# An FFN's up projection by seven block products instead of eight, with weight sums from accumulating DMAs and from VectorE

## The reference

```
def swiglu(x, w_in, w_out):
    gate, up = jnp.split(x @ w_in, 2, axis=-1)
    return (jax.nn.silu(gate) * up) @ w_out

h = swiglu(rmsnorm(x, g[0]), lw['ffn_in'][0], lw['ffn_out'][0])
x = x + FFN_RES * rmsnorm(h, g[1])
```

## Time and profile before

| | us |
|---|---|
| median of 3 runs (lowest, highest) | 2800.34 (2798.26, 2802.26) |
| the profiled execution | 2801.57 |
| its span, first to last instruction | 2799.8 |
| TensorE busy | 2723.5 |
| VectorE busy | 1254.4 |
| ScalarE busy | 888.7 |
| GpSimd busy | 383.1 |

### The profile page before, as it was taken

One profiled execution on the slowest core, in us unless ns is written; L12 is line 12 of the kernel. 1 busy time (PEld: TensorE's weight loads), 2 busy tenths in 40 slices (PEclk: granted clock), 3 DMA queues, 4 the chain that ended last, 5 costly groups with the idle time before them and its releaser, 6 DMA issues.

```text
span 2799.8 us, 45262 instructions
## 1 busy us (share of the span) xinstructions
PE 2723.5 (97%) x18703; PEld 2610.4 (93%) x18703; DVE 1254.4 (45%) x1697; ACT 888.7 (32%) x1213; POOL 383.1 (14%) x350
## 2 busy tenths in 40 slices
PE   8999999999899999999999999999989999999999
PEld 8999999997679999999999999999966899999998
...
DMA packets 367939, 191.19 MB, mean 68 GB/s; under 512 B 36477, under 2 KB 363472, under 8 KB 367822
## 3 DMA queue, kind: packets, MB, share of 16 engines
...
## 4 chain that ended last, share of the span: by engine, by line
PE 90%; DVE 5%; ACT 3%; issue 2%; DMA 0%; DVEq 0%; ACTq 0%; SPq 0%
PE ps L600 26%; PE ps L601 26%; PE ps L602 26%; PE ps L895 2%; PE ps L904 1%; PE ps L1023 1%; DVE w L1820 1%; PE ps L955 1%; ACT w L1323 1%; PE ps L1001 1%; DVE at L2118 1%; PE ps L937 1%; PE ps L1002 0%; DVE mx L2086 0%; DVE y L1913 0%
## 5 line engine op out<-in xcount | busy, mean ns | idle before, releaser
L600 PE MATMUL ps<-xh,w 128*128 128x320 f32 x3456 | 1076.3, 311 | 20.1 <-DVE xl L1897 13.3
L601 PE MATMUL ps<-xl,w 128*128 128x320 f32 x3456 | 1070.8, 310 | 0.0
L602 PE MATMUL ps<-xh,w 128*128 128x320 f32 x3456 | 1070.8, 310 | 0.0
L600 PEld LDWEIGHTS ps<-xh,w 128*128 128x128 f32 x3456 | 651.4, 188 | 29.5 <-DVE xl L1897 20.4
L601 PEld LDWEIGHTS ps<-xl,w 128*128 128x128 f32 x3456 | 651.7, 189 | 0.3
L602 PEld LDWEIGHTS ps<-xh,w 128*128 128x128 f32 x3456 | 651.4, 188 | 0.0
L1820 DVE TENSOR_TENSOR w<-raw,w 128x2048 fp32r<-128x2048 f32 x172 | 401.9, 2336 | 367.4 <-ACT w L1323 367.3
L1323 ACT ACTIVATE w<-raw 128x2048 fp32r<-128x2048 f32 (+2 forms) x185 | 342.6, 1852 | 414.6 <-PE ps L602 406.8
L600 PE MATMUL ps<-hh,w 128*128 128x320 f32 x1408 | 436.9, 310 | 1.0 <-DVE w L1820 1.0
L602 PE MATMUL ps<-hh,w 128*128 128x320 f32 x1408 | 435.1, 309 | 0.0
L601 PE MATMUL ps<-hl,w 128*128 128x320 f32 x1408 | 435.1, 309 | 0.0
...
## 6 DMA issues: line engine op xcount, KB each, us to landing
...
y<-in_cache_ckv_dram POOLq DMA_DIRECT2D x8, 256.0 KB, 3.2
```

The lines of the kernel that those rows point to most:

```text
L600: pe.matmul(out, wh, xh, start=first, stop=False)
L601: pe.matmul(out, wh, xl, start=False, stop=False)
L602: return pe.matmul(out, wl, xh, start=False, stop=last)
```

## The change

The up projection is cut into block products. For 128 columns, the weights of gate and up and the two halves of the features form a 2 x 2 matrix of blocks: A11 and A12 are gate's features 0 to 511 and 512 to 1023, A21 and A22 those of up (each 128x512 in SBUF). The activations form the other: features by token halves. `strassen_unit` computes the four results (gate and up, by token half) from seven products of blocks instead of eight, each 4 chunks x 3 = 12 matmuls of 128x320, so 84 for a unit instead of 96. In this it needs four sums of weight blocks and four combinations of activation blocks.

- *Weight sums.* S3 = A21 + A11 is made in RAW and S1 = A21 + A22 in SB (into which SP loads A21 once more), both by accumulating DMAs from SBUF to SBUF that GpSimd issues (`summed`). S2 and S4 are made on VectorE (`block_sum`). `group_hi` and `group_lo` split the seven blocks (3584 columns where a unit had 2048) in five groups: A11; S1 and S2; A12 and S3; A22; S4. Events: `ss_sb` for a sum, `ph_sb` for a high part, `pl_sb` for a low part, `pd_ps` for a product, `pc_sb` for a copy, `pu_sb` for VectorE's three steps on the results.
- *Results.* Products 1, 3 and 5 run up in bank b = 4j+1, where ScalarE first copies product 1, from PSUM to PSUM (COPY_P1); it copies the state of b behind products 3 and 5 out to GB and UB. Bank c takes product 2 and, once VectorE has made C22 = c + UB from it, product 7. The second half of gate is finished after product 7, in the next unit: gate_2, gate_2_r, Silu, `gated` (the product of both, with its sign), `high_h` (the copy into HH), `low_h`.
- *Activations.* `g_of_x` puts gain x X of four chunks into Y on ScalarE, behind r. `combined` makes three combinations and T4 from it on VectorE in units 1 and 2 of the plain part, split into TC; T4 is split into XH and XL (`fourth_hi`, `fourth_lo`) during the following down units. R is no longer applied to up: in the plain part the eviction of up multiplies with Silu's output, in place of two instructions.
- *Parts.* An FFN is now 4 plain up units and 8 down units over 4 chunks, then three times 6 block-product units and 8 down units over 6 chunks. All down parts start both of their first units before the last hidden chunk is there. The down weights of units 0 and 1 are split ahead. In the last down unit the sums of squares stand two chunks before its end instead of four.
- *Norm.* SY starts from a term for epsilon that ScalarE computes (`seed_y`) ahead of the last down units, instead of from GpSimd's memset; the logarithm takes no bias.
- Some semaphores of the mixers are merged.

```diff
-UP_A, UP_B = 12, 10
+PARTS = (4, 6, 6, 6)
+HT, HMAX = sum(PARTS), max(PARTS)
...
+QUARTERS = KD // 2
+BLK = QUARTERS * P
+PRODUCTS = ((0, True), (2, True), (1, False), (0, False), (1, False), (3, True), (2, False))
+LASTP = len(PRODUCTS) - 1
+GROUPS = (slice(0, 1), slice(1, 3), slice(3, 5), slice(5, 6), slice(6, 7))
+FREED_BY = (0, 2, 4, 5)
+G_A11, G_S12, G_A12S3, G_A22, G_S4 = range(5)
+STRASSEN = HT - PARTS[0]
+COPY_P1, COPY_U2, COPY_U3 = range(3)
+GATE_1, C22, C21 = range(3)
...
+            if blocks is not None:
+                for q in range(2 * pairs):
+                    i, j, g = q // 2, q % 2, blocks + q
+                    at = (first + q) * P
+                    load(unit(l, base, i, j), j,
+                         [(RAW[:, j, r * 1024:(r + 1) * 1024].rearrange("p (k n) -> p k n", n=P),
+                           src[:, :, at + r * DFF:at + r * DFF + P]) for r in range(2)])
+                    if q:
+                        sp.wait_ge(*pl_sb.nth(l, 4 * (g - 1) + G_S12))
+                    sp.dma_start(SB[:, 0, :].rearrange("p (k n) -> p k n", n=P),
+                                 src[:, 0:QUARTERS, at + DFF:at + DFF + P]).then_inc(loads_in, 16)
+                return
...
+        def strassen_unit(l, u, j, g):
+            pe.wait_ge(drained, u + 1)
+            for s, (bank, fresh) in enumerate(PRODUCTS):
+                if s == 0:
+                    pe.wait_ge(*pl_sb.nth(l, 4 * g + G_A11))
+                if s == 1:
+                    pe.wait_ge(*pl_sb.nth(l, 4 * g + G_S12))
+                if s == 2:
+                    pe.wait_ge(*pc_sb.nth(l, 3 * g + COPY_P1))
+                if s == 3:
+                    pe.wait_ge(*pl_sb.nth(l, 4 * g + G_A12S3))
+                if s == 4:
+                    pe.wait_ge(*pc_sb.nth(l, 3 * g + COPY_U2))
+                if s == 5:
+                    pe.wait_ge(lo_ready, u + 3)
+                if s == 6:
+                    pe.wait_ge(*pl_sb.nth(l, 4 * g + G_S4 - 1))
+                    pe.wait_ge(*pu_sb.nth(l, 3 * g + C22))
+                for k in range(QUARTERS):
+                    mm = three(PS[:, 4 * j + bank, 0:HALF], *slot_w(s, k), *product_x(s, k),
+                               fresh and k == 0, k == QUARTERS - 1, True)
+                mm.then_inc(unit_done if s == LASTP else pd_ps.sem, 1)
...
+        def strassen_up(l, f, p, base):
+            at, n = base + PART_AT[p], PARTS[p]
+            h0 = f * HT + sum(PARTS[:p])
+            def gate_2(q):
+                act.wait_ge(*gate_ready.nth(l, h0 + q))
+                run(GB[:, q % 2, N2], GB[:, q % 2, N2], ACT.Silu).then_inc(silu_ready.sem, 1)
+            for q in range(n):
+                j, g = q % 2, strassen(f, p, q)
+                more = q + 1 < n
+                b = PS[:, 4 * j + 1, 0:HALF]
+                if q:
+                    group_hi(l, at, q, g, G_S4)
+                act.wait_ge(*pd_ps.nth(l, LASTP * g))
+                run(b, PS[:, 4 * j, 0:HALF], ACT.Copy).then_inc(pc_sb.sem, 1)
+                if q:
+                    gate_2(q - 1)
+                if more:
+                    group_hi(l, at, q + 1, g + 1, G_A11)
+                if q:
+                    high_h(l, 1 - j, q - 1, h_ready.nth(l, g - 1))
+                act.wait_ge(*pd_ps.nth(l, LASTP * g + 2))
+                act.wait_ge(*hl_ready.nth(l, h0 + q - 2))
+                run(GB[:, j, N2], b, ACT.Copy).then_inc(pc_sb.sem, 1)
+                if more:
+                    group_hi(l, at, q + 1, g + 1, G_S12)
+                else:
+                    split_hi_d(l, at + n, 0, 0, n)
+                act.wait_ge(*pd_ps.nth(l, LASTP * g + 4))
+                run(UB[:, j, N1], b, ACT.Copy).then_inc(pc_sb.sem, 1)
+                act.wait_ge(*pu_sb.nth(l, 3 * g + GATE_1))
+                run(GB[:, j, N1], GB[:, j, N1], ACT.Silu)
+                if more:
+                    group_hi(l, at, q + 1, g + 1, G_A12S3)
+                    group_hi(l, at, q + 1, g + 1, G_A22)
+                else:
+                    split_hi_d(l, at + n, 0, 1, n)
+            gate_2(n - 1)
+            high_h(l, (n - 1) % 2, n - 1, h_ready.nth(l, strassen(f, p, n - 1)))
...
+        def g_of_x(l, f):
+            for c in range(QUARTERS):
+                run(Y[:, c, :], X[:, c, :], ACT.Copy, scale=gain(l, 32 * f + c)).then_inc(xc_act.sem, 1)
...
-            up(l, base, UP_A // 2, h0, True)
-            down(l, base + UP_A)
-            up(l, base + UP_A + DOWN, UP_B // 2, h0 + UP_A, False)
-            logarithms()
-            down(l, base + UP_A + DOWN + UP_B, 2 * f)
-            last = unit(l, base + UP_A + DOWN + UP_B, DOWN // 2 - 1, 1)
+                act.wait_ge(stored, (l + 1) * (16 * LAYER_STORES))
+            g_of_x(l, f)
+            plain_up(l, f, base)
...
+        def block_sum(l, at, q, g, n):
+            a11, a12 = (RAW[:, q % 2, b * BLK:(b + 1) * BLK] for b in range(2))
+            s1, s2 = SB[:, 0, :], SB[:, 1, :]
+            if n == S2:
+                dve.wait_ge(*arrived(s1_sum, l, g))
+                if q:
+                    dve.wait_ge(*pl_sb.nth(l, 4 * (g - 1) + G_S12))
+                V.scalar_tensor_tensor(out=s2, in0=s1, scalar=-1.0, in1=a11, op0=ALU.mult, op1=ALU.subtract)\
+                    .then_inc(ss_sb.sem, 1)
+            else:
+                dve.wait_ge(*ss_sb.nth(l, 2 * g + S2))
+                if q:
+                    dve.wait_ge(*pl_sb.nth(l, 4 * (g - 1) + G_S4 - 1))
+                V.tensor_tensor(S4[:, :], a12, s2, ALU.subtract).then_inc(ss_sb.sem, 1)
+        def gated(l, j, h, g):
...
+        def strassen_up(l, f, p, base):
+            at, n = base + PART_AT[p], PARTS[p]
+            h0 = f * HT + sum(PARTS[:p])
+            def gate_2(q):
+                j, u = q % 2, unit(l, at, 0, q)
+                dve.wait_ge(unit_done, u + 3)
+                V.tensor_tensor(GB[:, j, N2], PS[:, 4 * j + 2, 0:HALF], GB[:, j, N2], ALU.add).then_inc(drained, 1)
+            def gate_2_r(q):
+                j, u = q % 2, unit(l, at, 0, q)
+                dve.wait_ge(drained, u + 3)
+                V.tensor_tensor(GB[:, j, N2], GB[:, j, N2], R[:, N2], ALU.mult).then_inc(gate_ready.sem, 1)
+            for q in range(n):
+                j, g, u = q % 2, strassen(f, p, q), unit(l, at, 0, q)
+                more = q + 1 < n
+                a, b, c, d = (PS[:, 4 * j + bank, 0:HALF] for bank in range(4))
+                if q:
+                    gate_2(q - 1)
+                if q:
+                    gate_2_r(q - 1)
+                    group_lo(l, at, q, g, G_S4)
+                if q:
+                    gated(l, 1 - j, h0 + q - 1, g - 1)
+                if more:
+                    block_sum(l, at, q + 1, g + 1, S2)
+                    group_lo(l, at, q + 1, g + 1, G_A11)
+                    block_sum(l, at, q + 1, g + 1, S4_)
+                    group_lo(l, at, q + 1, g + 1, G_S12)
+                else:
+                    split_lo_d(l, at + n, 0, 0, n)
+                dve.wait_ge(*pd_ps.nth(l, LASTP * g + 3))
+                V.tensor_tensor(GB[:, j, N1], a, R[:, N1], ALU.mult).then_inc(pu_sb.sem, 1)
+                dve.wait_ge(*pc_sb.nth(l, 3 * g + COPY_U3))
+                V.tensor_tensor(UB[:, j, N2], c, UB[:, j, N1], ALU.add).then_inc(pu_sb.sem, 1)
+                dve.wait_ge(*pd_ps.nth(l, LASTP * g + 5))
+                V.tensor_tensor(UB[:, j, N1], UB[:, j, N1], d, ALU.subtract).then_inc(pu_sb.sem, 1)
+                if more:
+                    group_lo(l, at, q + 1, g + 1, G_A12S3)
+                    group_lo(l, at, q + 1, g + 1, G_A22)
+            gate_2(n - 1)
+            split_lo_d(l, at + n, 0, 1, n)
+            gate_2_r(n - 1)
+            gated(l, (n - 1) % 2, h0 + n - 1, strassen(f, p, n - 1))
...
+        def plain_up(l, f, base):
+            n, h0 = PARTS[0], f * HT
+            for k in range(n):
+                j, u = k % 2, unit(l, base, 0, k)
+                if k == 2:
+                    split_lo(l, base, 1, 1)
+                if k == 3:
+                    split_lo_d(l, base + n, 0, 0, n)
                 dve.wait_ge(unit_done, u + 3)
                 V.tensor_tensor(two(GB[:, j, :]), PS[:, 4 * j:4 * j + 2, 0:HALF], two(R[:, :]), ALU.mult)\
                     .then_inc(gate_ready.sem, 1)
-                dve.wait_ge(*hl_ready.nth(l, 2 * i + (h0 + j - 2)))
-                V.tensor_tensor(two(UB[:, j, :]), PS[:, 4 * j + 2:4 * j + 4, 0:HALF], two(R[:, :]), ALU.mult)\
+                dve.wait_ge(*silu_ready.nth(l, h0 + k))
+                dve.wait_ge(*hl_ready.nth(l, h0 + k - 2))
+                V.tensor_tensor(two(UB[:, j, :]), PS[:, 4 * j + 2:4 * j + 4, 0:HALF], two(GB[:, j, :]), ALU.mult)\
                     .then_inc(drained, 1)
-                dve.wait_ge(drained, u + 3)
-                dve.wait_ge(*silu_ready.nth(l, 2 * i + (h0 + j)))
-                V.tensor_tensor(UB[:, j, :], GB[:, j, :], UB[:, j, :], ALU.mult).then_inc(h_ready.sem, 1)
-
-            if first:
```

(44 more changed lines are left out.)

349 lines of the change are left out of this document (247 added, 102 removed).

## The result

The changed kernel takes **3181.3 us** (3176.2 to 3189.1, four runs) against 2800.8 for the kernel before on the same chip: a ratio of 1.136 (95% interval 1.1335 to 1.1389). The profiled execution took 3176.2 us with a span of 3174.4, 374.6 us more than that of before. The forecast was 2930 in 2840 to 3070: the direction and the place of the loss were right, the size was not, and the time lies outside the range. A third of the loss was foreseen.

The account below looks back on a forecast made before the run. TensorE was taken to bound the kernel. With the saving included, 73.2 + 22.4 + 17.2 + 8.8 + 6.3 = 127.9 us of net loss on 2801.6 gave 2930 us, range 2840 to 3070.

Parts of the forecast that it names:

- What is saved: Up projections: 72 units of 84 matmuls take 12.31 us instead of 14.08, saving 127.5 us if nothing waits.
- The loop that the change closes: Middle units: low_h, the DMAs, VectorE's sums and product 7 in a row take 12.79 + L each; +73.2 us.
- L: Time from issue to landing of a unit's second accumulating DMA; taken as 3.7 us, with bounds 1.9 and 5.3.
- The first rival: Accumulating DMAs also read their destination: L = 5.8, +266 us, 3068 us in all; chance 0.20.
- The third rival: The DMA adds far slower than it copies: L = 8 or more, over 3180 us; chance 0.04.
- product 7 "is 1.76 long": Last product of a block-product unit: its 12 matmuls take 1.76 us, at 0.1467 us each.
- Parts 2 and 3 ... cost nothing: Starts of parts 2 and 3: 15.84 us of down units cover a chain of some 13.9 us, so no loss.
- The case L = 5.3: Slow end of the forecast: +234 us, 3036 in all, with 17 for eight late first units of parts 2 and 3.
- The start of part 1: First sums wait for RAW: 4.4 us, and 1.2 more in the next unit, four times; +22.4 us.
- The start of an FFN: ScalarE's g_of_x copies delay the drain of unit 0, so TensorE waits 4.3 us, four times; 17.2 us.
- Plain up to down: Part 0's down unit 1 waits for weights split behind the last eviction chain: +2.2 us, four times; 8.8 us.
- hide under matmuls: Down phases: RAW loads and down splits (0.82 + 0.96 of 5.28 us on VectorE) cost nothing.

Follow-up runs that it names:

- e6: Changed kernel with all four weight sums on VectorE, without the accumulating DMAs and the extra load into SB: 2774.7 us, ratio 0.991.
- e1: Changed kernel with both accumulating DMAs put ahead of low_h in GpSimd's queue: 2890.6 us, ratio 1.033.
- e2: Changed kernel with 26 matmuls that nothing reads on TensorE ahead of product 7 in the middle units: 3097.6 us, ratio 1.106.
- e4: Changed kernel with plain copies in place of the two accumulating DMAs, so its output is not the FFN's: 3043.9 us, ratio 1.087.
- e9: Sums on VectorE and g_of_x behind the first Silu, plus the split ahead of the square in part 3's down phase: 2747.3 us, ratio 0.981.

## Why the prediction was right and wrong

- **"What is saved": right.** Units with nothing to wait for take 12.32 us (e6), the last units of a part mostly 12.3 in the changed kernel.
- **"The loop that the change closes": the mechanism right, shown by e1; its L mis-sized.** 12.79 + L holds to 0.02 us (e2). L was 4.27, not 3.7: 48 x 0.57 = 27 us. I built it of a fixed 2.15 and twice 1.05 of moving, from a DRAM load. e4 shows two errors of opposite sign: a copy within SBUF lands in 2.3, the second of two in 2.57, less than that sum gives, and the adding, for which it has nothing, costs 1.0 and 1.7 on top. The first rival was right that a sum costs more than a copy; its size, 5.8, is excluded by the runs, and its reason is not shown. The third rival's "over 3180" is near the measured 3181.3 by chance: it needed L = 8.
- **The step that failed most: product 7 "is 1.76 long".** Every term used the pitch of 0.147. The forecast itself put stalls of 4.2 us on TensorE in 48 units. In each the granted clock falls to 0.50, and TensorE then takes product 7 and much of product 1 at half speed: 73 us, shown by e2. This is also why the range was too narrow at its upper end. The trace of before could have given the price. The text ahead of the forecast calls the clock full in the FFNs, and it is not at their starts: in three of the four, after short stalls (1.68 us of waiting up to 927.56 in the second), 11 to 19 matmuls run at 0.267, some 6 us in all.

```profile
929.00:931.00 2.00, 1.97 (x6) 0.50 0.00 0
```

```profile
929.44 0.47 PE L601 MATMUL ps<-xl,w 128*128 128x320 f32 x1
929.71 0.47 PE L602 MATMUL ps<-xh,w 128*128 128x320 f32 x1
```

- **"Parts 2 and 3 ... cost nothing": wrong.** From the last full unit of one part to the first of the next plus that last unit itself, 24.6 + 42.2 us of matmuls took 76.1: 9.2 lost, eight times, 74 us. Of this 1.4 each stay in e6; the rest goes with the DMAs. I gave their chain 13.9 of 15.84 us with the undisturbed landing; at part starts S1's sum takes 5.3 to 7.0 us beside the RAW load of the next unit (that this load is the cause, no run tests), and product 1 waits 2.1 to 3.0 us. And the forecast had unit q = 0 at 12.31, since its DMAs were issued before low_h(0): it did not see that the sum for unit 1 waits for SB to be free and loaded, which holds up C22 of unit 0 by the same order of VectorE. It counted this for part 1 alone, with 1.2 us; it costs 4.5 us in each of the twelve first units, 1.6 of it by the clock. The case L = 5.3 had 17 us here, so even there it was short.
- **"The start of part 1": +22.4, was about 42.** The changed kernel loses 33 us more than e6 up to the first unit's end, and e6 itself waits 9 (L2067, 2.3 each, behind the low part of T4). The causes are the same: 5.26 for 3.7, the second load of SB, and the clock.
- **"The start of an FFN": right.** 4.02 us each, forecast 4.3; 16.1 against 17.2.
- **"Plain up to down": short.** 2.93 + 0.83 us each, 15 against 8.8: VectorE's low part met low_h on GpSimd and took 1.7 instead of 0.68.
- **Down phases "hide under matmuls": not in part 3.** Square, split and a low part beside GpSimd's addition make 3.7 us before its third unit, plus the clock: 16 us, shown by e9. In parts 1 and 2 TensorE waits 1.1 us at the same place. Seeding SY was hidden, as said.
- **"The tail": near.** The wait for the squares rose from 4.7 to 9.5 us, 4.8 against 6.3.

The whole difference can be laid out by place. The table takes the starts of TensorE's matmuls in the traces, and counts in each place what their distances are longer than 0.1467 us, less the same in the kernel before. "Lowered pitch" are the distances between 0.16 and 0.36 us, most of them 0.267; what is left are waits. Down phases include the wait before the part behind them.

| place | forecast, us | changed kernel | of it lowered pitch | e6 |
|---|---|---|---|---|
| 864 matmuls fewer | -127.5 | -126.7 | | -126.7 |
| 48 middle units | 200.6 | 307.0 | 86.2 | 0.0 |
| 12 first units of a part | 4.8 | 53.9 | 19.6 | 6.5 |
| 12 last units of a part | 0 | 2.3 | 2.3 | 0.0 |
| 4 down phases of part 0 | 26.4 | 53.9 | 4.0 | 31.5 |
| 8 down phases of parts 1 and 2 | 0 | 31.7 | 0.8 | 11.1 |
| 4 down phases of part 3 | 6.3 | 23.1 | 6.1 | 27.8 |
| 4 x first two plain units | 17.2 | 15.5 | -1.8 | 13.9 |
| 4 x other two plain units | 0 | 8.2 | 7.4 | 9.7 |
| outside the FFNs' matmuls | 0 | 5.7 | | 2.7 |
| sum | 127.8 | 374.6 | 124.6 | -23.5 |

So half of the 247 us that the forecast lacks is the lowered clock, which it priced at nothing anywhere; the other half are waits, mostly at the starts of parts and in the 0.57 us of L. That the clock is the cause of its share is shown by an experiment for the middle units alone (e2); elsewhere it is counted, not tested.
